# The high halves of the feed-forward weights: from a ScalarE copy to a converting DMA on GpSimd's queue

## The reference

```python
h = rmsnorm(x, attn_norm)
proj = h @ w_in                       # 2048 x 4352
mix = [rmsnorm(dilated attention, 16 heads), rmsnorm(sliding-window attention, 16 heads)]
x = x + mix @ w_out                   # 2048 x 2048
h = rmsnorm(x, ffn_norm)
gate, up = h @ w_gate, h @ w_up       # 2048 x 5632 each
x = x + (silu(gate) * up) @ w_down    # 5632 x 2048
out = rmsnorm(x, final_norm)
```

## Time and profile before

| | |
|---|---|
| runs, median of 2 | 2178.3 us (2177.91 to 2178.68) |
| profiled execution, span from first to last instruction | 2177.5 us |
| its own time | the page gives the span alone |
| TensorE, VectorE, ScalarE, GpSimd busy | 99%, 47%, 34%, 5% of the span |
| data moved | 205.99 MB, mean 95 GB/s |

### The profile page before, as it was taken

How to read it: one execution, slowest core, us unless ns; L and a number is a source line. 1 busy time by engine, 2 the same in 40 slices (tenths; PEclk the granted TensorE clock), 3 DMA queues, 4 the chain that set the end, 5 groups by cost and what they waited for, 6 DMA issues and landing times.

```text
span 2177.5 us, 29367 instructions
## 1 busy us (share of the span) xinstructions
PE 2161.0 (99%) x9718; PEld 1767.6 (81%) x9718; DVE 1029.9 (47%) x1940; ACT 744.5 (34%) x1436; POOL 111.5 (5%) x191
## 2 busy tenths in 40 slices
PE   8999999999999999999999999999999999999998
PEld 7777777777888888888888888888888888888886
DVE  5455566556675534343343433434343343433435
ACT  5354555455423522222222222222222222222223
POOL 0012212112100000000000000000000000000000
PEclk9999999999999999999999999999999999999999
DMA  6222222223222333333333333333323333233333
GB/s 179 87 69 68 67 63 71 65 67 136 77 94 91 106 98 97 97 97 96 96 96 96 96 96 96 96 96 96 96 96 96 96 96 96 96 96 97 96 97 130
DMA packets 300437, 205.99 MB, mean 95 GB/s; under 512 B 12336, under 2 KB 266592, under 8 KB 299872
## 3 DMA queue, kind: packets, MB, share of 16 engines
q1 hardware_dynamic: 297168, 198.82, 30.0%
q10 hardware_dynamic: 3216, 6.47, 0.8%
HBM read 201.05 MB, written 4.19 MB: 94 GB/s over the span
## 4 chain that ended last, share of the span: by engine, by line
PE 97%; DVE 1%; issue 1%; ACT 1%; SPq 0%; DMA 0%; POOLq 0%; POOL 0%; ACTq 0%
PE bank L284 21%; PE bank L286 21%; PE bank L285 21%; PE bank L331 9%; PE bank L333 9%; PE bank L332 9%; PE bank L346 2%; PE bank L345 1%; PE bank L361 1%; PE bank L378 1%; PE bank L377 1%; DVE h_lo L880 0%; DMA raw<-in_w_in 0%; SPq L250 0%; DVE w_lo L876 0%
## 5 line engine op out<-in xcount | busy, mean ns | idle before, releaser
L876 DVE TENSOR_TENSOR w_lo<-raw,w_hi 128x512 fp32r<-128x512 f32 x716 | 496.9, 695 | 1067.8 <-ACT w_hi L599 1066.9
L599 ACT ACTIVATE w_hi<-raw 128x512 fp32r<-128x512 f32 x716 | 451.2, 631 | 1209.5 <-PE bank L286 792.0
L284 PE MATMUL bank<-h_hi,w_hi 128*128 128x512 f32 x1952 | 770.8, 395 | 0.9 <-DVE h_lo L880 0.9
L286 PE MATMUL bank<-h_hi,w_lo 128*128 128x512 f32 x1952 | 760.8, 390 | 0.0
L285 PE MATMUL bank<-h_lo,w_hi 128*128 128x512 f32 x1952 | 760.2, 389 | 0.0
L284 PEld LDWEIGHTS bank<-h_hi,w_hi 128*128 128x128 f32 x1952 | 366.5, 188 | 79.3 <-DVE h_lo L880 1.7
L286 PEld LDWEIGHTS bank<-h_hi,w_lo 128*128 128x128 f32 x1952 | 366.4, 188 | 78.0
L285 PEld LDWEIGHTS bank<-h_lo,w_hi 128*128 128x128 f32 x1952 | 366.8, 188 | 73.0
L331 PE MATMUL bank<-w_hi,act_hi 128*128 128x512 f32 x896 | 350.8, 391 | 0.4 <-DVE x_res L1108 0.2
L333 PE MATMUL bank<-w_hi,act_lo 128*128 128x512 f32 x896 | 348.9, 389 | 0.0
L332 PE MATMUL bank<-w_lo,act_hi 128*128 128x512 f32 x896 | 348.7, 389 | 0.0
(11 more groups left out here) (130 smaller groups left out, 1140.5 us busy)
## 6 DMA issues: line engine op xcount, KB each, us to landing
raw<-in_w_gate SPq DMA_DIRECT2D x176, 256.0 KB, 2.9
raw<-in_w_up SPq DMA_DIRECT2D x176, 256.0 KB, 2.9
raw<-in_w_down SPq DMA_DIRECT2D x176, 256.0 KB, 2.4
raw<-in_w_in SPq DMA_DIRECT2D x136, 256.0 KB, 2.9
raw<-in_w_out SPq DMA_DIRECT2D x64, 256.0 KB, 2.5
x_first<-in_x SPq DMA_DIRECT2D x8, 512.0 KB, 7.8
x_res<-in_x ACTq DMA_DIRECT2D x4, 1024.0 KB, 10.3
out_x<-x_res SPq DMA_DIRECT2D x3, 1024.0 KB, 3.9
```

Of the source, the lines that this page charges most:

```text
L284: nc.tensor.matmul(out_ap, st_hi, mv_hi, start=start, stop=False, skip_group_check=True)
L286: return nc.tensor.matmul(out_ap, st_lo, mv_hi, start=False, stop=stop, skip_group_check=True)
L599: nc.scalar.activation(w_hi[:, s, :], raw[:, s, :], ACT.Copy).then_inc(w_hi_done, 1)
L876: nc.vector.tensor_tensor(w_lo[:, s, :], raw[:, s, :], w_hi[:, s, :].bitcast(F32), ALU.subtract).then_inc(w_lo_done, 1)
```

## The change

In the feed-forward stage ScalarE no longer copies. `w_hi[:, s]` is filled by a second DMA of the same weights, float32 in HBM to fp32r in SBUF, that GpSimd issues (`load_hi`) once TensorE has used the slot. It has semaphores of its own, one for each slot (`hi_loaded`). VectorE's `split` waits for both loads. The converting loads are 516: units 0 to 31 of the 11 steps, the 16 down units of ten steps, and four of the last step's. The 12 that go into `h2_hi` keep ScalarE's copy. The first three feed-forward units are split during the out-projection's last slots, as before, so there too ScalarE skips its copy and VectorE passes `ffn=True`. GpSimd's third `invert` now stands behind the sixth load.

```diff
@@ semaphores
+    hi_loaded = [sem(f"hi_loaded{i}") for i in range(RING)]
@@ ScalarE, out-projection
             for s in range(16):
-                split(*ahead(U_OUT // 4 + 4 * g + s // 4, s % 4))
+                if g < 3 or s < 16 - AHEAD:
+                    split(*ahead(U_OUT // 4 + 4 * g + s // 4, s % 4))
@@ ScalarE, ffn and the last split
             for s in range(32 if last else 48):
-                split(*ahead(U_FFN // 4 + 12 * i + s // 4, s % 4))
...
-        split(u4, AHEAD)
@@ VectorE
-        def split(u4, s):
-
-            dve.wait_ge(w_hi_done, 4 * u4 + s + 1)
+        def split(u4, s, ffn=False):
+
+            if ffn:
+                dve.wait_ge(raw_loaded[s], 16 * (u4 + 1))
+                dve.wait_ge(hi_loaded[s], 16 * (u4 - U_FFN // 4 + 1))
+            else:
+                dve.wait_ge(w_hi_done, 4 * u4 + s + 1)
             nc.vector.tensor_tensor(w_lo[:, s, :], raw[:, s, :], w_hi[:, s, :].bitcast(F32), ALU.subtract).then_inc(w_lo_done, 1)
@@ VectorE, the callers
-                split(*ahead(u4 + s // 4, s % 4))
+                split(*ahead(u4 + s // 4, s % 4), ffn=g == 3 and s >= 16 - AHEAD)
...
-                split(*ahead(U_FFN // 4 + 12 * i + s // 4, s % 4))
+                split(*ahead(U_FFN // 4 + 12 * i + s // 4, s % 4), ffn=True)
...
-        split(u4, AHEAD)
+        split(u4, AHEAD, ffn=True)
...
-            dve.wait_ge(w_hi_done, 4 * u4 + j + 1)
+            dve.wait_ge(w_hi_done, U_FFN + j - 3)
@@ GpSimd
         invert(2, slice(0, 2 * NT))
-        invert(3, slice(0, NT))
+
+        def load_hi(u4, s, src):
+            pool.wait_ge(w_used, 4 * u4 + s - 3)
+            dst = w_hi[:, s, :]
+            if len(src.shape) == 3:
+                dst = dst.rearrange("p (k c) -> p k c", c=P)
+            nc.gpsimd.dma_start(dst, src).then_inc(hi_loaded[s], 16)
+
+        def tall(w, j, col):
+            return w[512 * j:512 * (j + 1), bass.ds(col, P)].rearrange("(k p) c -> p k c", p=P)
+
+        def ffn(i, first=False, last=False):
+            u4 = U_FFN // 4 + 12 * i
+            for s in range(32):
+                load_hi(u4 + s // 4, s % 4, tall((w_gate2, w_up2)[s // 4 % 2], s % 4, i * 512 + P * (s // 8)))
+                if first and s == 5:
+                    invert(3, slice(0, NT))
+            for n in range(1 if last else NC):
+                for k in range(4):
+                    load_hi(u4 + 8 + n, k, w_down2[bass.ds(i * 512 + P * k, P), 512 * n:512 * (n + 1)])
+
+        ffn(0, first=True)
+        for i in range(1, STEPS_F):
+            ffn(i, last=i == STEPS_F - 1)
```

## The result

The changed kernel took 2231.57 us, median of two runs (2230.13 and 2233.01), against 2178.3. The ratio is 1.0244, 95% interval 1.0225 to 1.0263. The forecast was 2225 us, in a range of 2195 to 2480. The profiled run is the one of 2230.13 us; its span is 2228.2 us, 50.7 more than before.

A forecast was written before the change was run, and what follows sets the result against it. TensorE, busy 99% of the span, was taken as the bound. Its added waits, 36 + 4 + 3.3 + 3.6 = 47 us, on top of 2178.3 gave 2225 us, +2.1%, in a range of 2195 to 2480.

The forecast's parts named there:

- (a): Each step's end: VectorE's bank addition stands behind the subtraction; TensorE waits T less 1.4, 3.6 us, ten times: 36 us.
- (c): The stage's start: the four h_lo operations stand behind the subtraction for unit 5, 3.3 us later; TensorE's gap costs that.
- (d): The end, last step: the subtraction after unit 32 starts, and the chain to act_lo behind it, come 3.6 us later.
- T: Time from TensorE freeing a slot to VectorE's subtraction for its next content: 0.87 us before, forecast 4.97 tall, 4.47 wide.
- wake-up: Term of T: GpSimd's delay after TensorE frees the slot, taken as 0.20 us like ScalarE's.
- Contention: Term of T: a high load meeting the raw-load stream on the DMA engines lands 0.87 us later.
- GpSimd's part: Term of T: what GpSimd takes to issue a transfer, taken as 1.0 us; no row showed it.
- the power operation: GpSimd's small operation, 1.01 us for 128x4 elements, read as nearly all fixed cost; basis for the 1.0 us issue term.
- (b): Each step's fourth act_lo, behind slot 33's subtraction: T may be 4.1; 4.47 costs 0.4 us, ten times: 4 us.
- The clock: Rival: after each of ten stalls one unit runs at 1.2 GHz, 27 us more, 2252 us; within the forecast's 0.37.
- quick enough: Rival: GpSimd's issue overlaps or streams don't meet; T 3.1 to 4.85, 2208 us, not slower by 2%; chance 0.29.
- The rate rival: Rival: GpSimd's queue can't keep one load per 2.72 us unit, so units stretch; 2285 to 2900 us, chance 0.28.

The follow-up runs named there:

- e1: The changed kernel with VectorE adding the first bank of each step's last down group before the waiting subtraction in slot 47, not after: 2197.8 us.
- e3: The kernel before, no DMA changed, with an extra ScalarE copy of about 1.8 us ahead of w_hi copies in slots 36 to 47, steps 1 to 9: 2193.4 us.
- e7: e6 with VectorE also doing TensorE's needed work ahead of the waiting subtractions at the stage's start and end, all 516 converting loads kept: 2180.7 us.
- e2: The kernel before, ScalarE still copying, plus 480 converting loads on GpSimd's queue into a spare tile that nobody reads: 2178.5 us.
- e8: The kernel before with the ballast loads of e2, but float32 to float32, without conversion: 2178.6 us in one run.
- e6: e1 with ScalarE's 1 MB load of g_fin issued before the last step, not at the stage's start: 2191.1 us.
- e5: The changed kernel with ten matmuls into a free bank before TensorE waits for x_res at each of ten step boundaries: 2223.5 us.
- e4: The changed kernel with a GpSimd pass over 128x1024 floats ahead of each converting load, unit 8 of step 0 to unit 31 of the last: 2250.7 us.

## Why the prediction was right, and where it wasn't

**The path** was right. TensorE, not ScalarE, is the bound; the copies were free to remove; the loads keep the rate; and TensorE waits for what stands behind VectorE's subtraction. e1, e3 and e7 show it from three sides, e2 rules out the traffic by itself. Signs (a), (c), (d) all came, between boundaries units keep their 2.72 us. The DMA share is 0.76, above the 0.64 foretold: converting packets cost more than plain ones (e8).

**T was too long**: 4.97 foretold, 4.15 measured. The wake-up is 0.45 us, not 0.20 (1002.16 to 1002.62). Contention is 0.3 us, not 0.87: tall raw loads land in 3.2 us, before in 2.9. GpSimd's part is 0.5 us beyond SyncE's (3.7 against 3.2), not the 1.0 taken from the power operation. 0.45 + 2.9 + 0.3 + 0.5 = 4.15. The power operation was misread besides: the trace of before has it at 0.54 us for 128x1, 1.01 for 128x4 and 1.66 for 128x8, so it is not nearly all fixed cost. The Trainium skill (DMA: Bandwidth & Descriptors, Latency and other measured facts) has about 0.4 us between the two paths' first bytes. The 0.5 us of the tall loads is near it, but the wide ones show no difference (2.9 us by either queue), so here it is no fixed price of the path.

**(a)** 36 us foretold, 28.5 measured: the law held to 0.13 us, T was off. **(b)** 4 foretold, none measured: the wide T, 0.45 + 2.9 = 3.4, stayed below its 4.1. **(d)** 3.6 foretold, 2.45 measured: 2.85 less the 0.4 of before.

**(c)** 3.3 foretold, 7.8 measured: 8.5 less the 0.6 of before. Two things were missed: g_fin's 1 MB in front of TensorE's needs (e6), and a first gap of 1.3 us before unit 0, since the h_lo operations of slot 15 stand behind a subtraction too.

**The clock** was a rival with 27 us and part of the 0.37, and the forecast's sum had nothing for it. It took 13 us, half of the 27: five of the ten gaps, and those at the start and the end, were followed by matmuls at 1.2 GHz. Why these five stays open: four of them have the longest gaps (2.88 to 3.00 us), but the fifth has the shortest (2.64). The Trainium skill (TensorE: Matmul & The Clock Gate, Part 1) says that the array falls back to 1.2 GHz when idle. The windows at 0.50 agree, and e5 shows that work in the gap keeps the clock up.

So 2225 came near 2231.6 partly by errors that cancel. With the true T the prediction's own sum would be 27.5 + 0 + 2.5 + 2.5 = 32.5, 2211 us, the rival "quick enough": its T, 3.1 to 4.85, is what happened, and its verdict, within 2%, is not, because of 13 us of clock and 5 us more at the start. That the time fell into the forecast's own range is luck to this extent. **The rate rival** (0.28) was wrong: GpSimd is occupied 0.74 us per tall load, and with 1.84 us (1.05 + 0.79, e4) it still kept the rate.

## What to carry to other kernels

When a supply gets slower, don't only ask whether it still comes before its consumer needs it. Look at the in-order engine that waits for it and list what stands behind the wait; the slack is that of the tightest item there, here 1.27 us and not the 7.4 of the subtraction itself. A wait belongs behind everything that the bound engine needs: swapping two instructions gave back 34 of 53 us. And relieving an engine that the bound engine hides is worth nothing, whatever its busy time says.

## What the runs showed of the hardware

- GpSimd's DMA instruction takes 0.74 us for a tall load of 512 pieces and 0.53 us for a wide one of 128, SyncE's 0.37 and 0.33: if the 384 further pieces make the difference, they cost GpSimd an estimated 0.55 ns each.
- Converting loads of 256 KB make five times as many packets as plain ones from the same queue, and the engines 1.5 times as busy (27.8% against 18.7%), with the same 3.4 us to landing for tall ones (e2, e8).
- After gaps of 1.5 us in TensorE's work the clock never fell (nine gaps, e3), after 2.6 to 3.0 us in five of ten cases, after 3.3 to 3.7 us in nine of ten (e4). With ten matmuls put into each of the boundaries' gaps it never fell behind them (ten gaps, e5).
- With a transfer of 1 MB issued 0.8 us behind it, a converting load of 256 KB let VectorE start 7.8 us after its issue, and without the transfer 3.4 us after it (changed kernel, e6).
- Beside passes of GpSimd over 128x1024 floats, 16 of 508 of VectorE's subtractions and 19 of 44 of its products act_s took over 0.75 us, up to 1.6, instead of 0.69 (e4); beside GpSimd's DMA instructions alone none did (changed kernel).
